# Full-precision router logits, one-pass ranks and an eight-bank first gather in a two-layer trunk

## The chip, the cores and the metric

One core of a Trainium2 chip. Five engines work side by side: TensorE (PE, matmul), VectorE (DVE), ScalarE (ACT), GpSimd (POOL) and SyncE (SP, which issues the weight DMAs). The metric is the device time of one execution in microseconds.

## What is computed

Two pre-norm residual layers over 256 tokens of width 1024. Each has a mixer of four branches and then a channel mixer: dense in layer 0, in layer 1 a top-2-of-8 mixture of experts. The change lies between the mixer of layer 1 and its first expert:

```python
def moe_swiglu(h, w_router, b_router, w_gate, w_up, w_down):
    xt = h.reshape(T, D)                      # h = RMSNorm(x), T = 256, D = 1024
    logits = (xt @ w_router).astype(jnp.float32) + b_router.astype(jnp.float32)
    top_logit, top_e = lax.top_k(logits, TOP_K)          # 2 of 8
    top_w = jax.nn.softmax(top_logit, axis=-1)
    ...
    # tokens sorted by expert; for expert e: (silu(xb @ w_gate[e]) * (xb @ w_up[e])) @ w_down[e]
    out = jnp.zeros((T, D), h.dtype).at[row_tok].add(ys * row_w[:, None].astype(ys.dtype))
```

## The kernel before

Tokens lie in two tiles of 128 (m). Nearly every product runs as three float32r products of a high and a low part (`mm3`, L390 to L392): weights land in a ring of SBUF slots by SP's DMAs (L416), ScalarE rounds each half of a piece to `whi` (`split_hi`, L371), VectorE subtracts for `wlo` (`split_lo`, L378), and six buffers of each are in turn. One half is six instructions of 512 columns on TensorE. Activations are treated alike: PSUM to `hTh` on ScalarE, the difference `hTl` on VectorE. Each engine runs its own list in program order, and semaphores join the lists.

Between the mixer and the experts of layer 1 the lists are these.

- `token_norm(3, ...)` on VectorE (L1511, L1513) adds the mixer's result to x and multiplies by the gain, in four quarters (m, g); TensorE turns each quarter (`transposed_h`, L588); ScalarE makes `hTh` (L1162) and the sums of squares (L1157), VectorE `hTl` (L1488). Then ScalarE takes the root (L1181), which loads an activation table first.
- `router()` on TensorE multiplies a 16-column matrix (router weights, high and low) with hTh and hTl (L954, L956, L959), ScalarE copies the result `lgT` out (L1451), a product with `fold` turns and adds the two halves (L965). VectorE adds the bias (L1884), finds the two largest of eight (L1888, L1895), compares indices (`hot`, L1900), and adds them to `member` columns in `tab` (L1902). Five float32 products with triangular and full ones give each token its rank within its expert and the counts (L972 to L976). VectorE copies them (L1906, L1907) and makes `pick`, 1 where a token's rank equals the column, one instruction per token tile and expert (`pick_tokens`, L2059).
- `first_gather()` multiplies the tokens (`htokh` from ScalarE, L1454, and `htokl` from VectorE, `token_lower`, L1911) with `pick`: 32 instructions of 256 columns (128 slots of each of two experts) into four banks (L982). Each bank, with two of the eight k, is copied by ScalarE (`gathered_upper`, L1425) and VectorE (`gathered_lower`, L2073).
- `expert_pass(0, 0, 0)` then runs: gate, up and down pieces in the order g0 g0 u0 u0 g1 g1 ..., with `act` (L2006) turned on TensorE (`turn`, L1086) after the second gate step has begun.

`idle_products` (L581) are products whose result nobody reads; they stand where TensorE would be empty. `link` in a list makes the engine wait for its own last instruction.

## Time and profile before

| | |
|---|---|
| time, median of 3 executions | 1021.17 us (1021.12 to 1021.25) |
| profiled execution, first to last instruction | 1019.3 us |
| TensorE busy | 1006.4 us, 99% |
| VectorE busy | 810.6 us, 80% |
| granted TensorE clock, mean | 1.000 |
| DMA | 257.13 MB, 252 GB/s |

The profile is one further execution with the hardware profiler; its own time is known as the span, and the runs without it are 1.9 us longer than that, which is what lies around the first and last instruction. A busy time is the union of an engine's instructions, and matmul ends are modelled and overlap the next start, so steps on TensorE are read from start to start. In a timeline row the first number is the start, the second the time until the end of the last of the merged instructions; in brackets stands how long the engine was idle before, and who ended that.

### The profile page before, as it was taken

How to read it: one execution, taken by the hardware profiler on the slowest of the kernel's cores; microseconds unless marked ns; L12 is line 12 of the kernel's file. 1: busy time of each engine (PE TensorE's matmuls, PEld its weight loads, DVE VectorE, ACT ScalarE, POOL GpSimd, SP SyncE). 2: the span in 40 equal slices, each digit the busy share in tenths (PEclk: the TensorE clock that was granted, in tenths of full speed). 3: DMA queues.
4: the chain of work that ended last, by engine and by line, in shares of the span. 5: the costliest groups of instructions: out<-in, count | busy, mean ns of one | idle time of the engine just before them, and what ended most of it. 6: DMA issues, size and time to landing. Idle time of an engine off the chain costs nothing.

```text
span 1019.3 us, 14045 instructions
## 1 busy us (share of the span) xinstructions
PE 1006.4 (99%) x4954; PEld 850.9 (83%) x4954; DVE 810.6 (80%) x1108; ACT 649.8 (64%) x890; POOL 38.3 (4%) x87
## 2 busy tenths in 40 slices
PE   7999999999999999999999999999999999999998
PEld 6888888888888888888888888888888988898887
DVE  5799888665645455699888858999889988989898
ACT  6657655555534343756674548787877787868775
POOL 6000000040000000100000000000000000000020
PEclk9999999999999999999999999999999999999999
DMA  9834555687455654843555556999999999999995
GB/s 273 247 113 165 162 182 169 210 242 244 168 185 191 203 170 136 284 148 121 192 160 192 186 171 217 337 373 382 364 340 395 380 364 352 391 371 356 361 394 200
DMA packets 117700, 257.13 MB, mean 252 GB/s; under 512 B 5216, under 2 KB 29858, under 8 KB 117648
## 3 DMA queue, kind: packets, MB, share of 16 engines
q1 hardware_dynamic: 113344, 243.55, 68.4%
q0 software_dynamic: 3296, 9.22, 3.1%
q10 hardware_dynamic: 1008, 3.67, 0.9%
q8 instruction: 32, 0.52, 0.2%
q14 instruction: 20, 0.16, 0.0%
HBM read 249.08 MB, written 7.34 MB: 252 GB/s over the span
## 4 chain that ended last, share of the span: by engine, by line
PE 88%; DVE 6%; ACT 3%; DMA 2%; issue 1%; SPq 0%; DVEq 0%; ACTq 0%
PE bank L390 27%; PE bank L392 26%; PE bank L391 26%; DVE wlo L378 2%; DMA ring<-in_w_in 2%; ACT whi L371 1%; DVE dacc L1723 1%; PE bank L1086 1%; PE bank L1009 1%; PE bank L1008 1%; PE bank L674 1%; DMA ring<-in_moe_w_gate 1%; PE bank L664 1%; PE bank L912 0%; PE bank L689 0%
## 5 line engine op out<-in xcount | busy, mean ns | idle before, releaser
L378 DVE TENSOR_TENSOR wlo<-ring,whi 128x1024 fp32r<-128x1024 f32 (+2 forms) x506 | 541.5, 1122 | 104.4 <-ACT whi L371 102.1
L371 ACT CAST whi<-ring 128x1024 fp32r<-128x1024 f32 (+2 forms) x506 | 463.3, 971 | 96.0 <-PE bank L392 79.0
L390 PE MATMUL bank<-whi,hTh 128*128 128x512 f32 (+3 forms) x992 | 375.4, 378 | 1.7 <-DVE wlo L378 0.9
L392 PE MATMUL bank<-whi,hTl 128*128 128x512 f32 (+3 forms) x992 | 370.4, 373 | 0.0
L391 PE MATMUL bank<-wlo,hTh 128*128 128x512 f32 (+3 forms) x992 | 370.1, 373 | 0.0
L390 PEld LDWEIGHTS bank<-whi,hTh 128*128 128x128 f32 x992 | 186.4, 188 | 32.0 <-issue 2.3
L392 PEld LDWEIGHTS bank<-whi,hTl 128*128 128x128 f32 x992 | 186.4, 188 | 29.1
L391 PEld LDWEIGHTS bank<-wlo,hTh 128*128 128x128 f32 x992 | 186.5, 188 | 28.3 <-issue 0.5
L390 PE MATMUL bank<-whi,oTh 128*128 128x512 f32 x392 | 155.4, 396 | 0.1
L392 PE MATMUL bank<-whi,oTl 128*128 128x512 f32 x392 | 153.1, 391 | 0.0
L391 PE MATMUL bank<-wlo,oTh 128*128 128x512 f32 x392 | 152.9, 390 | 0.0
L390 PEld LDWEIGHTS bank<-whi,oTh 128*128 128x128 f32 x392 | 73.7, 188 | 15.7 <-DVE wlo L378 0.7
L392 PEld LDWEIGHTS bank<-whi,oTl 128*128 128x128 f32 x392 | 73.6, 188 | 15.7
L391 PEld LDWEIGHTS bank<-wlo,oTh 128*128 128x128 f32 x392 | 73.7, 188 | 14.4
L1723 DVE SCALAR_TENSOR_TENSOR dacc<-zpad,cw,dacc 128x256 f32<-128x256 f32 x120 | 49.0, 480 | 0.0
L1250 ACT ACTIVATE gsig<-bank,rstd 128x512 f32<-128x512 f32 x32 | 20.3, 685 | 35.6 <-PE bank L392 35.4
L1383 ACT CAST oTh<-bank 128x512 fp32r<-128x512 f32 (+1 forms) x24 | 13.2, 551 | 39.2 <-PE bank L1086 39.1
L1361 ACT CAST oTh<-bank 128x512 fp32r<-128x512 f32 x11 | 6.0, 590 | 29.0 <-PE bank L912 29.0
L572 POOL DMA_INDIRECT htokh<-yrows,trowi x2 | 2.2, 1107 | 568.5 <-DVE trowi L1982 568.2
L1849 DVE SCALAR_TENSOR_TENSOR act<-bank,rstd,sig 128x512 f32<-128x512 f32 (+1 forms) x12 | 7.9, 702 | 17.6 <-PE bank L392 17.6
L1858 DVE TENSOR_TENSOR oTl<-bank,oTh 128x512 fp32r<-128x512 f32 x11 | 7.1, 687 | 18.5 <-ACT oTh L1361 18.5
L1999 DVE TENSOR_TENSOR oTl<-bank,oTh 128x512 fp32r<-128x512 f32 (+1 forms) x24 | 15.4, 643 | 7.1 <-ACT oTh L1383 6.9
(333 smaller groups left out, 678.9 us busy)
## 6 DMA issues: line engine op xcount, KB each, us to landing
ring<-in_w_in SPq DMA_DIRECT2D x40, 1024.0 KB, 5.2
ring<-in_moe_w_down SPq DMA_DIRECT2D x40, 1024.0 KB, 7.0
ring<-in_moe_w_gate SPq DMA_DIRECT2D x32, 1024.0 KB, 6.9
ring<-in_moe_w_up SPq DMA_DIRECT2D x32, 1024.0 KB, 7.8
ring<-in_moe_w_gate SPq DMA_DIRECT2D x16, 768.0 KB
ring<-in_moe_w_up SPq DMA_DIRECT2D x16, 768.0 KB, 7.2
ring<-in_ffn_w_gate SPq DMA_DIRECT2D x11, 1024.0 KB, 5.1
ring<-in_ffn_w_up SPq DMA_DIRECT2D x11, 1024.0 KB, 5.1
```

What stands on the lines that cost most here:

```text
L371: nc.scalar.copy(whi[pc.part(hf)][:, 0:n], pc.raw[:, hf * n:(hf + 1) * n]).then_inc(hi_done, 1)
L378: nc.vector.tensor_tensor(wlo[q][:, 0:n], pc.raw[:, hf * n:(hf + 1) * n], whi[q][:, 0:n].bitcast(F32), ALU.subtract).then_inc(lo_done, 1)
L390: nc.tensor.matmul(o, sh, wh, start=start, stop=False)
L391: nc.tensor.matmul(o, sh, wl, start=False, stop=False)
L392: return nc.tensor.matmul(o, sl, wh, start=False, stop=stop)
L664: nc.tensor.matmul(bank[4 + hd][:, P:384], q[:, P:T], k[:, 0:T], start=True, stop=True).then_inc(sc_mm, 1)
L674: last = nc.tensor.transpose(bank[4 + hd][:, P * j:P * (j + 1)], probs[:, hd, P * j:P * (j + 1)], ident[:, :])
L1008: nc.tensor.matmul(o, htokh[:, m, c], pick[:, m, :, :], start=(m == 0), stop=False)
L1250: nc.scalar.activation(gsig[:, j % 2, m, :], bank[2 + m][:, :], ACT.Sigmoid, scale=rstd[:, 1, m:m + 1]).then_inc(gate_sig, 1)
L1383: nc.scalar.copy(eaTh[st % 2][:, 0:n], bank[4][:, 0:n]).then_inc(e_aT_hi, 1)
L1723: ins = V.scalar_tensor_tensor(out=dacc[:, c, :], in0=z, scalar=cw[:, c, j:j + 1], in1=dacc[:, c, :], op0=ALU.mult, op1=ALU.add)
L1999: V.tensor_tensor(eaTl[st % 2][:, 0:n], bank[4][:, 0:n], eaTh[st % 2][:, 0:n].bitcast(F32), ALU.subtract).then_inc(e_aT_lo, 1)
```

## The change

The router's logits are computed by plain float32 products from unsplit turned tokens (`hTf`), with tokens as output rows, so that neither the copy nor the fold is needed. `last_norm` takes the place of `token_norm(3, ...)` on ScalarE: the square root's table is loaded first, token tile 1's squares are summed in halves, and the PSUM copies are shared between ScalarE (three) and VectorE (two). Ranks use float32r matrices, and a token that is not a member gets its rank moved by -1024, so that no member factor is needed and the first pick is one comparison with the ranks in PSUM. The first gather writes each k to a bank of its own and is drained in eight steps. `tab` shrinks from six rows to four.

```diff
+FIRST_BANK = [2, 3, 5, 0, 1, 4, 7, 6]
+RANK0 = -1024.0
...
             def router():
-                idle_products(3)
-                pe.wait_ge(wr_lo, 1)
...
-                pe.wait_ge(lgT_ev, 1)
-                pe.wait_ge(iota_ready, 1)
-                for m in range(MT):
-                    last = nc.tensor.matmul(bank[6][:, 32 + 8 * m:40 + 8 * m], lgT[0:2 * NE, P * m:P * (m + 1)],
-                                            fold[0:2 * NE, :], start=True, stop=True)
-                last.then_inc(lgT_mm, 1)
-
-                idle_products(10)
+                def logits(m, g):
+                    pe.wait_ge(hTf_ready[m][g], 2 if m and g else 1)
+                    for k in range(4 * g, 4 * g + 4):
+                        last = nc.tensor.matmul(bank[2 + m][:, 0:NE], hTf[:, k, P * m:P * (m + 1)], wr[:, k, :],
+                                                start=(k == 0), stop=(k == KD - 1))
+                    if g:
+                        last.then_inc(lg_mm, 1)
+
+                transposed_h(3, [(0, 0), (0, 1), (1, 0)])
+                pe.wait_ge(router_in, 32)
+                logits(0, 0)
+                pe.wait_ge(h_ready, h_count(3, 1, 1))
+                for k in range(4, KD):
+                    last = nc.tensor.transpose(bank[1 if k < 6 else 7][:, P * (k % 2):P * (k % 2 + 1)],
+                                               hm[:, 1, P * k:P * (k + 1)], ident[:, :])
+                    if k % 2:
+                        last.then_inc(hT_mm, 1)
+                logits(0, 1)
+                logits(1, 0)
+                idle_products(2, 0)
+                logits(1, 1)
+                idle_products(8, 0)
+                pe.wait_ge(ranker_ready, 1)
                 pe.wait_ge(member_ready, 1)
-                mem = [tab[:, 2 + m, 0:NE] for m in range(MT)]
-                nc.tensor.matmul(bank[6][:, 0:8], upstrict[:, :], mem[0], start=True, stop=True)
-                nc.tensor.matmul(bank[6][:, 8:16], upstrict[:, :], mem[1], start=True, stop=False)
+                mem = [member[:, m, :] for m in range(MT)]
+                nc.tensor.matmul(bank[6][:, 0:8], ranker[:, :], mem[0], start=True, stop=True)
+                nc.tensor.matmul(bank[6][:, 8:16], ranker[:, :], mem[1], start=True, stop=False)
                 nc.tensor.matmul(bank[6][:, 8:16], ones[:, :], mem[0], start=False, stop=True)
                 nc.tensor.matmul(bank[6][:, 16:24], ones[:, :], mem[0], start=True, stop=False)
                 nc.tensor.matmul(bank[6][:, 16:24], ones[:, :], mem[1], start=False, stop=True).then_inc(rank_mm, 1)
-                idle_products(6)
+                idle_products(6, 0)
 
             def first_gather():
                 def product(k, tokens, m, start=False, stop=False):
-                    o = bank[(5, 6, 0, 1)[k // 2]][:, T * (k % 2):T * (k % 2) + T]
-                    return nc.tensor.matmul(o, tokens[:, m, P * k:P * (k + 1)], pick[:, m, :, :], start=start, stop=stop)
-
-                def opened(k):
-                    product(k, htokh, 0, start=True)
-                    product(k, htokl, 0)
-                    product(k, htokh, 1)
+                    return nc.tensor.matmul(bank[FIRST_BANK[k]][:, 0:T], tokens[:, m, P * k:P * (k + 1)],
+                                            pick[:, m, :, :], start=start, stop=stop)
 
                 pe.wait_ge(pick_ready, 1)
                 pe.wait_ge(tok_hi, 2)
+                for k in range(KD):
+                    if FIRST_BANK[k] == 6:
+                        pe.wait_ge(rank_read, 1)
+                    product(k, htokh, 0, start=True)
+                    product(k, htokh, 1)
                 pe.wait_ge(tok_lo, 1)
-                for part in range(4):
-                    opened(2 * part)
+                for k in range(KD):
+                    product(k, htokl, 0)
                 pe.wait_ge(tok_lo, 2)
-                for part in range(4):
-                    product(2 * part, htokl, 1, stop=True)
-                    opened(2 * part + 1)
-                    product(2 * part + 1, htokl, 1, stop=True).then_inc(gat_mm, 1)
+                for k in range(KD):
+                    product(k, htokl, 1, stop=True).then_inc(one_mm, 1)
...
-                    if side == 0 and st == 0:
-                        pe.wait_ge(gat_lo, 4 * q + 2 * part + 2)
+                    if side == 0 and st == 0 and not first:
+                        pe.wait_ge(gat_lo, 4 * q + 2 * part - 2)
                     for hf in range(2):
+                        if st == 0 and first:
...
             mixer(1)
-            transposed_h(3)
             router()
             first_gather()
-            idle_products(4)
             expert_pass(0, 0, 0)
...
+            def last_norm():
+                def turned_copy(m, g, n):
+                    act_e.wait_ge(hT_mm, h_count(3, m, g))
+                    nc.scalar.copy(hTf[:, 4 * g:4 * g + n, P * m:P * (m + 1)],
+                                   bank[h_bank(3, m, g)][:, 0:P * n].rearrange("p (k t) -> p k t", t=P)
+                                   ).then_inc(hTf_ready[m][g], 1)
+
+                nc.scalar.activation(stat[:, 62:63], eps[:, :], ACT.Sqrt)
+                act_e.wait_ge(x_new, 10)
+                nc.scalar.activation(esig, x[:, 0, :], ACT.Square, accum_out=ssum[:, 0:1])
+                act_e.wait_ge(x_new, 11)
+                link(nc.scalar.activation(eact[:, 0:512], x[:, 1, 0:512], ACT.Square, accum_out=ssum_half[:, 0:1]))
+                link(nc.scalar.activation(ssum_half[:, 1:2], ssum_half[:, 0:1], ACT.Identity, bias=eps[:, 0:1],
+                                          scale=1.0 / D))
+                turned_copy(0, 0, 4)
+                act_e.wait_ge(x_new, 12)
+                link(nc.scalar.activation(eact[:, 512:D], x[:, 1, 512:D], ACT.Square, accum_out=ssum[:, 1:2]))
+                nc.scalar.activation(rstd[:, 0, 0:1], ssum[:, 0:1], ACT.Sqrt, bias=eps[:, 0:1], scale=1.0 / D)
+                nc.scalar.activation(rstd[:, 0, 1:2], ssum[:, 1:2], ACT.Sqrt, bias=ssum_half[:, 1:2],
+                                     scale=1.0 / D).then_inc(rms_root, 1)
+                turned_copy(0, 1, 4)
+                turned_copy(1, 1, 2)
...
-            token_norm(3, after_mixer(1, 1))
-            act_e.wait_ge(lg_mm, 1)
-            nc.scalar.copy(lgT[0:2 * NE, :], bank[7][0:2 * NE, 0:T]).then_inc(lgT_ev, 1)
+            last_norm()
             act_e.wait_ge(rstd_ready, 4)
             for m in range(MT):
                 nc.scalar.mul(htokh[:, m, :], hm[:, m, :], rstd[:, 1, m:m + 1]).then_inc(tok_hi, 1)
             split_hi(act_e, after_mixer(1, 1))
             act_e.wait_ge(diff_ready, 1)
             nc.scalar.activation(wtop[:, :, :], diff[:, :, :], ACT.Sigmoid).then_inc(wtop_ready, 1)
-            for part in range(4):
-                gathered_upper(0, part, (5, 6, 0, 1)[part])
+            for k in range(KD):
+                act_e.wait_ge(one_mm, k + 1)
+                nc.scalar.copy(hTh[:, k, :], bank[FIRST_BANK[k]][:, 0:T]).then_inc(one_hi, 1)
             expert_pass(0, 0, 0)
             act_e.wait_ge(rounds_ready, 1)
...
                 elif k == 3:
-                    lower_hT(k, [(0, 0), (1, 0), (0, 1), (1, 1)])
+                    for done, b, first, n in ((15, 5, 0, 4), (17, 7, 6, 2)):
+                        dve.wait_ge(hT_mm, done)
+                        V.tensor_copy(hTf[:, first:first + n, P:2 * P],
+                                      bank[b][:, 0:P * n].rearrange("p (k t) -> p k t", t=P)
+                                      ).then_inc(hTf_ready[1][first // 4], 1)
...
             def router_prep():
                 dve.wait_ge(iota_ready, 1)
-                V.tensor_copy(iotaf[:, :], iotai[:, :])
+                link(V.tensor_copy(iotaf[:, :], iotai[:, :]))
+                V.tensor_scalar(marks[:, :], iotaf[:, :], RANK0, None, ALU.add)
                 V.memset(tab[:, :, :], 0.0)
-                dve.wait_ge(wr_hi, 1)
-                V.tensor_tensor(wrl, wr[:, :, :], wrh.bitcast(F32), ALU.subtract).then_inc(wr_lo, 1)
+                V.scalar_tensor_tensor(out=ranker[:, :], in0=ident[:, :], scalar=RANK0 - 1.0, in1=upper[:, :],
+                                       op0=ALU.mult, op1=ALU.add).then_inc(ranker_ready, 1)
 
             def router():
-                dve.wait_ge(lgT_mm, 1)
                 dve.wait_ge(rstd_ready, 4)
                 for m in range(MT):
-                    last = V.scalar_tensor_tensor(out=lg[:, m, :], in0=bank[6][:, 32 + 8 * m:40 + 8 * m],
-                                                  scalar=rstd[:, 1, m:m + 1], in1=rbias[:, :], op0=ALU.mult, op1=ALU.add)
+                    dve.wait_ge(lg_mm, m + 1)
+                    link(V.scalar_tensor_tensor(out=lg[:, m, :], in0=bank[2 + m][:, 0:NE], scalar=rstd[:, 1, m:m + 1],
+                                                in1=rbias[:, :], op0=ALU.mult, op1=ALU.add))
+                    link(V.max(top8[:, m, :], lg[:, m, :]))
+                    last = V.max_index(idx8[:, m, :], top8[:, m, :], lg[:, m, :])
                 link(last)
-                for m in range(MT):
-                    last = V.max(top8[:, m, :], lg[:, m, :])
-                link(last)
+                link(V.tensor_copy(idxf[:, :, :], idx8[:, :, 0:2]))
+                chosen = idxf[:, :, :].rearrange("p m s -> p s m")
+                link(V.tensor_tensor(hot[:, :, :, :],
+                                     iotaf[:, 0:NE].unsqueeze(1).unsqueeze(1).to_broadcast([P, 2, MT, NE]),
+                                     chosen.unsqueeze(3).to_broadcast([P, 2, MT, NE]), ALU.is_equal))
+                V.tensor_tensor(member[:, :, :], hot[:, 0, :, :], hot[:, 1, :, :], ALU.add).then_inc(member_ready, 1)
                 for s in range(2):
                     last = V.tensor_tensor(diff[:, :, s:s + 1], top8[:, :, s:s + 1], top8[:, :, 1 - s:2 - s],
                                            ALU.subtract)
                 last.then_inc(diff_ready, 1)
-                for m in range(MT):
-                    last = V.max_index(idx8[:, m, :], top8[:, m, :], lg[:, m, :])
-                link(last)
-                link(V.tensor_copy(idxf[:, :, :], idx8[:, :, 0:2]))
-                for s in range(2):
-                    for m in range(MT):
-                        last = V.tensor_scalar(hot[:, s, m, :], iotaf[:, 0:NE], idxf[:, m, s:s + 1], None, ALU.is_equal)
-                link(last)
-                V.tensor_tensor(tab[:, 2:4, 0:NE], hot[:, 0, :, :], hot[:, 1, :, :], ALU.add).then_inc(member_ready, 1)
-                token_lower(0)
-                dve.wait_ge(member_ready, 1)
                 dve.wait_ge(rank_mm, 1)
+                rank = bank[6][:, 0:2 * NE].rearrange("p (m e) -> p m e", m=MT)
+                V.tensor_tensor(pick[:, :, :, :], marks[:, :].unsqueeze(1).unsqueeze(1).to_broadcast([P, MT, 2, P]),
+                                rank[:, :, 0:2].unsqueeze(3).to_broadcast([P, MT, 2, P]),
+                                ALU.is_equal).then_inc(pick_ready, 1)
                 V.tensor_copy(cnt[:, :], bank[6][:, 16:24])
-                link(V.tensor_copy(tab[:, 0:2, 0:NE], bank[6][:, 0:16].rearrange("p (m e) -> p m e", m=MT)))
+                V.tensor_copy(tab[:, 0:2, 0:NE], rank).then_inc(rank_read, 1)
...
                 link(V.tensor_reduce(tpass[:, :, :], oprod[:, :, :, :], AX_X, ALU.add))
+                link(V.tensor_scalar(trank[:, :, :], trank[:, :, :], RANK0, None, ALU.subtract))
...
-                        member = tab[:, 2 + m, bass.ds(2 * q + side, 1)]
-                        last = V.tensor_scalar(pick[:, m, side, :], iotaf[:, :], rank, member, ALU.is_equal, ALU.mult)
+                        last = V.tensor_scalar(pick[:, m, side, :], marks[:, :], rank, None, ALU.is_equal)
...
             router()
-            pick_tokens(0)
-            token_lower(1)
-            split_lo(dve, after_mixer(1, 1), halves=(0,))
-            for part in range(4):
-                gathered_lower(0, part, (5, 6, 0, 1)[part])
+            for m in range(MT):
+                token_lower(m)
+            for k in range(KD):
+                if k == 4:
+                    split_lo(dve, after_mixer(1, 1), halves=(0,))
+                dve.wait_ge(one_hi, k + 1)
+                V.tensor_tensor(hTl[:, k, :], bank[FIRST_BANK[k]][:, 0:T], hTh[:, k, :].bitcast(F32),
+                                ALU.subtract).then_inc(one_lo, 1)
             split_lo(dve, after_mixer(1, 1), halves=(1,))
             router_weights()
```

The order on TensorE from the last transposes to the first expert weights, before (waits in brackets, rows that repeat left out):

```order
L588 MATMUL bank<-ident,h 128x128 [waits h_ready]
L588 MATMUL bank<-ident,h 128x128 x3
L581 MATMUL bank<-upper,ident 128x128 x3
L956 MATMUL bank<-hTh,wrp 16x256 [waits hT_lo,wr_lo]
L965 MATMUL bank<-fold,lgT 128x8 [waits iota_ready,lgT_ev]
L965 MATMUL bank<-fold,lgT 128x8
L581 MATMUL bank<-upper,ident 128x128 x10
L972 MATMUL bank<-tab,upstrict 128x8 [waits member_ready]
L581 MATMUL bank<-upper,ident 128x128 x6
L982 MATMUL bank<-pick,htokh 128x256 [waits tok_lo,tok_hi,pick_ready]
L581 MATMUL bank<-upper,ident 128x128 x4
L390 MATMUL bank<-whi_60,hTh 128x512 [waits lo_done,gat_lo]
```

and in the change (`L583` and `L956` are the transposes, `ym` holds the turned tokens):

```order
L946 MATMUL bank<-wr,ym 128x8 [waits hTf_ready00,router_in]
L946 MATMUL bank<-wr,ym 128x8 x3
L956 MATMUL bank<-ident,h 128x128 [waits h_ready]
L946 MATMUL bank<-wr,ym 128x8 [waits hTf_ready01]
L946 MATMUL bank<-wr,ym 128x8 [waits hTf_ready10]
L576 MATMUL bank<-upper,ident 128x128 x2
L946 MATMUL bank<-wr,ym 128x8 [waits hTf_ready11]
L576 MATMUL bank<-upper,ident 128x128 x8
L968 MATMUL bank<-member,ranker 128x8 [waits member_ready,ranker_ready]
L576 MATMUL bank<-upper,ident 128x128 x6
L977 MATMUL bank<-pick,htokh 128x256 [waits tok_hi,pick_ready]
L394 MATMUL bank<-whi_60,hTh 128x512 [waits lo_done,one_lo]
```

The first logits now stand ahead of the last four transposes, and the idle products lie around the last logits.

VectorE, from the ranks to the sixth low half, before:

```order
L1906 COPY cnt<-bank 128x8 [waits rank_mm,member_ready]
L1907 COPY tab<-bank 128x2x8
L2059 TENSOR_SCALAR pick<-iotaf,tab 128x128 [waits dve_seq]
L2059 TENSOR_SCALAR pick<-iotaf,tab 128x128 x3
L1911 SCALAR_TENSOR_TENSOR htokl<-h,rstd,htokh 128x1024 [waits tok_hi]
L378 TENSOR_TENSOR wlo_68<-ring_56,whi_62 128x1024 [waits hi_done]
L2073 TENSOR_TENSOR hTl<-bank,hTh 128x512 [waits gat_hi] x4
L378 TENSOR_TENSOR wlo_69<-ring_56,whi_63 128x1024 [waits hi_done]
```

and in the change:

```order
L1920 TENSOR_TENSOR pick<-marks,bank 128x512 [waits rank_mm]
L1923 COPY cnt<-bank 128x8
L1924 COPY tab<-bank 128x2x8
L1928 SCALAR_TENSOR_TENSOR htokl<-h,rstd,htokh 128x1024 [waits tok_hi] x2
L2120 TENSOR_TENSOR hTl<-bank,hTh 128x256 [waits one_hi] x4
L382 TENSOR_TENSOR wlo_68<-ring_56,whi_62 128x1024 [waits hi_done]
L2120 TENSOR_TENSOR hTl<-bank,hTh 128x256 [waits one_hi] x4
L382 TENSOR_TENSOR wlo_69<-ring_56,whi_63 128x1024 [waits hi_done]
```

Both token halves moved behind the comparison, and the low weight half `wlo_68` from ahead of the drain into its middle.

## Rows read from the trace of the kernel before

**Rows 1.** The page: span, and TensorE's busy tenths in 40 slices.

```profile
span 1019.3 us, 14045 instructions
...
PE   7999999999999999999999999999999999999998
```

**Rows 2.** Windows: length, busy us and instructions of PE, PEld, DVE, ACT, POOL, clock, DMA.

```profile
612.40:629.40 17.00, 15.47 (x126) 13.79 (x124) 13.43 (x38) 12.97 (x20) 0.00 (x0) 1.00 0.59 221
629.40:643.10 13.70, 13.70 (x63) 11.28 (x63) 13.48 (x18) 11.50 (x12) 0.00 (x0) 1.00 0.79 284
```

**Rows 3.** The chain of waits: start us, us, what.

```profile
616.93 1.28 ACT L1181
...
619.43 2.43 PE bank L581 x20
...
623.46 1.12 DVE pick L2059 x4
...
624.62 4.10 PE bank L982 x32
```

**Rows 4.** Timeline of PE, from the fold products to the gather.

```profile
618.82 0.61 PE L965 MATMUL bank<-fold,lgT 16*128 16x8 f32 x4 [0.73 <-ACT lgT L1451]
...
621.78 0.39 PE L972 MATMUL bank<-tab,upstrict 128*128 128x8 f32 x2
622.03 0.37 PE L973 MATMUL bank<-tab,upstrict 128*128 128x8 f32 x2
...
622.92 1.58 PE L581 MATMUL bank<-upper,ident 128*128 128x128 f32 x12
```

**Rows 5.** Timeline of DVE, from the last h to the tokens' low part.

```profile
613.84 0.69 DVE L1513 TENSOR_TENSOR h<-x,gain 128x512 f32<-128x512 f32 x1
...
619.47 0.36 DVE L1884 SCALAR_TENSOR_TENSOR lg<-bank,rstd,rbias 128x8 f32<-128x8 f32 x2 [0.75 <-PE bank L965]
...
620.49 0.16 DVE L1895 FIND_INDEX8 idx<-top,lg 128x8 uint32<-128x8 f32 x1
620.68 0.17 DVE L1897 CAST idxf<-idx 128x4 f32<-128x4 uint32 x1
...
621.55 0.18 DVE L1902 TENSOR_TENSOR tab<-hot 128x16 f32<-128x16 f32 x1
...
624.49 1.28 DVE L1911 SCALAR_TENSOR_TENSOR htokl<-h,rstd,htokh 128x1024 fp32r<-128x1024 f32 x1
```

**Rows 6.** Timeline of ACT: copies, root, first copy of the gather.

```profile
613.04 1.56 ACT L1162 CAST hTh<-bank 128x512 fp32r<-128x512 f32 x3 [0.70 <-PE bank L588]
...
618.22 0.30 ACT L1181 ACTIVATE rstd<-ssum,eps 128x2 f32<-128x2 f32 x1
...
626.96 2.39 ACT L1425 CAST hTh<-bank 128x512 fp32r<-128x512 f32 x4 [2.62 <-PE bank L982]
```

**Rows 7.** Timeline of DVE, from the drain to the first activation product.

```profile
627.58 2.49 DVE L2073 TENSOR_TENSOR hTl<-bank,hTh 128x512 fp32r<-128x512 f32 x4 [0.68 <-ACT hTh L1425]
629.99 1.22 DVE L378 TENSOR_TENSOR wlo<-ring,whi 128x1024 fp32r<-128x1024 f32 x1
...
631.91 9.41 DVE L378 TENSOR_TENSOR wlo<-ring,whi 128x1024 fp32r<-128x1024 f32 x8
641.24 0.68 DVE L2006 TENSOR_TENSOR act<-sig,bank 128x512 f32<-128x512 f32 x1
```

**Rows 8.** Groups by line and form, ACT: count, busy us, mean ns, idle before.

```profile
L1402 ACT CAST pickT<-bank 128x256 fp32r<-128x256 f32 x1 | 0.4, 373 | 2.1 <-PE bank L1018 2.1
```

**Rows 9.** Timeline of PE: the first weights and the first expert transposes.

```profile
629.37 0.47 PE L390 MATMUL bank<-whi,hTh 128*128 128x512 f32 x1
...
643.09 0.60 PE L1086 MATMUL bank<-ident,act 128*128 128x128 f32 x4
```

**Rows 10.** Timeline near the end, DVE and PE's weight load.

```profile
979.22 0.17 DVE L1969 TENSOR_SCALAR tover<-trank 128x4 f32<-128x4 f32 x1
...
1002.90 0.19 PEld L390 LDWEIGHTS bank<-whi,oTh 128*128 128x128 f32 x1 [0.42 <-DVE wlo L378]
```

79 lines of the change are left out of this document (29 added, 50 removed).

## The prediction

> **What bounds the kernel now.** I read the page first: a span of 1019.3 us and a TensorE row that is full in every slice but the first and the last [rows 1]. Such a row hides short holes, so I then took the two stretches around the change by windows [rows 2]. From 612.4 to 629.4 TensorE computes no weights at all: it transposes, routes, gathers and runs idle products. This 17.0 us is the only place that the change can shorten much. From 629.4 to 643.1 TensorE is busy for all of 13.7 us, and VectorE for 13.48 of them. That second number matters more than the first: whatever is won before 629.4 must be followed by a VectorE that has 0.2 us to spare.
>
> The granted clock is 1.00 in both stretches. Ten half pieces of six weight products each fill 629.37 to 643.09 [rows 9], 1.37 us for one.
>
> **What is removed or moved.** Square-root table load: 1.28 us stood between the second square sum and the root [rows 3]. In the change it is issued before any x of this norm is ready, where ScalarE idles. The chain through 16-row logits, their copy to SBUF and the fold products is gone; so are four hTh/hTl splits that only served the router. Ten rank instructions become five. Four picks (1.12 us) and two copies ahead of them become one comparison. Four idle products before the first weights go, two are added between the logits, two fewer stand before the ranks. Against this stand 16 new logit products in float32, two instructions each if they act as the old rank products [rows 4], and a gather that is drained in eight narrow steps instead of four wide ones.
>
> **The new chain, on the old trace's clock.** Up to the last h, which ends at 614.53 [rows 5], nothing changes.
>
> - ScalarE: the first half square of token tile 1 can start at 612.51, when its x is ready; with the accumulator read it ends at 613.2. A small activation (0.2, taken like the root's 0.30 less one column and a wait) and the copy of (0,0), 0.59 as in [rows 6], end at 614.07. The second half square, its read and two roots (each starts 0.2 after the one before [rows 6]) end at 615.1, the copy of (0,1) at 615.70.
> - TensorE: logits (0,0) from 614.12. Eight instructions at 0.112: the old rank products with 8 columns start 0.25 apart once and 0.22 afterwards, for two instructions [rows 4]. They end at 615.02, so the last four transposes, which could go at 614.58 before, wait 0.44 behind them. (0,1) must wait for the copy and starts at 615.75; (1,0) follows at once; 16 instructions, to 617.54. Two idle products, 0.53. (1,1) from 618.07, the last instruction at 618.85 and its result at 619.10.
> - VectorE then does the token tile 1 alone, since tile 0 is done by 617.5: logits 0.22, maximum 0.17, match and find 0.23, cast 0.17, one comparison of 32 columns 0.19, member 0.18 [rows 5], and 0.03 to 0.04 at each of five waits. Member stands at 620.5.
> - Idle products: eight are 16 instructions. In the old chain 20 such instructions took 2.43 us, 0.121 each [rows 3], so they occupy TensorE until 620.9. They run 0.35 us longer than what they bridge.
> - Ranks: 5 x 0.112, the last result at 621.60. The comparison of 512 columns from PSUM is bounded by 0.68 (one subtraction of this size from PSUM, [rows 7]) and by 1.12 (the four old picks, [rows 3]). I take 0.69, since it is one instruction of the same shape: ready at 622.4. But six idle products take 1.42 [rows 4] and hold TensorE until 622.9. Another 0.5 us of waiting that the change makes itself.
> - Gather: 24 instructions at 0.12 (32 took 4.1 us in the chain, [rows 3]) before the first bank gets its last one: 625.86, result 626.14. The two low halves of the tokens, 1.28 each [rows 5], now both stand behind the comparison and end at 624.9, in time.
> - First copy out of PSUM: at 626.18, where the old one started at 626.96 [rows 6]. **Here the gain is 0.8 us**, although the route to it looks much shorter.
>
> **The drain and what it does to VectorE.** A copy of 256 columns is 0.37 on ScalarE [rows 8]; the first low part starts at 626.57. On VectorE the start-to-start time is 0.60 for 512 columns and 1.14 for 1024 [rows 7]; that is 0.067 per instruction and 1.04 ns per column, so 0.333 for 256. TensorE needs two of the eight: it starts weights at 627.37 against 629.37 [rows 9], **2.0 us earlier**. VectorE however must do all eight and one weight half between them, 8 x 0.333 + 1.14 = 3.8 us, and so reaches the next half at 630.37. It was 629.99 before: 0.4 us *later*. Its small weight columns (1.92 from that start to the next half) are the same in both, so the eight halves that began at 631.91 begin at 632.29. There was one wait of 0.14 among them, on a ScalarE that is now ahead; without it the activation product, 641.24 before, starts at 641.47 and ends at 642.15. The first expert transposes need it. They ran at 643.09 [rows 9]; now they can run at 642.20.
>
> So TensorE, 2.0 us ahead at first, loses 0.2 at the fourth half, 0.5 at the fifth (634.9 before, which is 629.37 and four halves; it could start at 632.9 and its low half ends at 633.5), and 0.4 at the transposes. **What is left is 0.9 us.** Behind them every half has over 2 us in hand in the old trace, so this shift lasts: TensorE has no idle time to give or lose until the end.
>
> At the end the change adds one small VectorE operation with a wait, 0.19 us, ahead of 979.22 [rows 10]. VectorE is nearly full from there to 1002.90, where TensorE waits for a low half. I book 0.1 us (0 to 0.19; a wait of 0.14 in front of that half may take it up). The extra constants of the first layer and the removed pool work lie where TensorE does not wait for them; nothing. Dropping the member factor changes no duration: both forms read at least one scalar column.
>
> Sum: 0.9 - 0.1 = 0.8 us off the profiled execution, span 1018.5 for 1019.3. The runs show 1021.17, that is 1.9 more than the span, in a spread of 0.13; with the same offset 1020.4. About 0.2% (2.0 us) is what a measurement of this kernel can tell from no change.
>
> The Trainium skill has a rule against the eight narrow steps. "VectorE: DVE Perf Modes", section on the TRN2 errata, charges every operation a fixed latency (120 cycles from PSUM) and advises tiles of 512 or more. By its table eight steps of 256 columns cost 0.5 us more than four of 512, and the sum would fall to an estimated 0.6 us. Above, rows of this case give 0.27 for the same difference, and the sum goes by them.
>
> **Rivals.**
>
> - *VectorE does not hold TensorE, and the idle products do not overhang.* Speaks for it: 2.0 us at the first weights is a plain result, and both overhangs (0.35 + 0.5) are estimates from 0.121 per instruction. Against: VectorE was busy 13.48 of 13.70 us [rows 2]. If the full head start survives, 2.0 + 0.85 - 0.1 = 2.75: 1018.4. With only the overhangs gone and VectorE still in the way, 1.65: 1019.5, inside my range. 0.11.
> - *TensorE's clock falls (slower).* Between 615.7 and 622.4 the change leaves TensorE 24 instructions with 8 columns each, 5 rank ones and idle products; before, most of this time held products with 256 columns. For it: the columns per us are the lowest of this whole stretch. Against: the old trace has a hole of 0.73 us and then 8-column instructions here [rows 4], at a granted clock of 1.00 [rows 2]. If the clock drops to 1.2 GHz at logits (1,1) and is back for the gather, 8 + 16 + 5 + 12 instructions cost twice: +0.9 +1.9 +0.6 +1.4 = 4.8 us, 1025.2. It decides the sign from about 8 such instructions on, and is measurable from 25. 0.08.
>   The Trainium skill, "TensorE: Matmul & The Clock Gate", in its part on PE-mode transpose, says that a transpose does not count as busy for the clock gate in the way a product does; by that rule the fall would be likelier and its price the same. No row decides it: the old trace has 16 transposes in this stretch at a clock of 1.00.
> - *The change does not do what it says.* The comparison with two broadcast operands, one in PSUM, or the accumulator reads with their waits cost more than their nearest rows, by 0.5 us or more together. Then VectorE starts the eight halves a whole microsecond late and nothing is left: 1021.0 to 1021.5. 0.08.
>
> **How the numbers follow.** Forecast 0.73: 0.3 (0.121 for all small instructions, tail 0.19) to 1.7 us off. The range 1019.2 to 1021.3 holds this and most of the last rival, and leaves out the first two, 0.19. Faster by over 0.2% is the first rival, 0.11; slower is the clock, 0.08; all else is within 0.2%, 0.81.
>
> **What would show it.** In the new profile: no table load before the root; first weights near 627.4 but the first expert transposes only near 642.2; before them TensorE waits for VectorE at the low halves and at the activation product; idle products directly followed by ranks and by the gather, without a wait on member or pick. I am wrong if TensorE does not wait between 627 and 643, or if the granted clock of 612 to 629 is under 1.

## Result and profile after

The change is slower by 0.23%: 1022.99 us against 1020.83 (medians of 12 each), a ratio of 1.0023 with an interval of 1.0016 to 1.0030. The forecast was 1020.4 in 1019.2 to 1021.3, "within 0.2%". The 12 times lie between 1020.86 and 1025.94, those of before between 1020.08 and 1021.25. That spread is the first hint: with each time comes a mean granted clock of TensorE, and it goes from 0.998 (1020.9 to 1022.0 us) down to 0.993 (1025.5 and 1025.9 us); with the kernel before it is 1.000.

The page of the profiled execution (1023.08 us) has it in one digit of the clock's row, in the slice of the change:

```profile
span 1021.3 us, 14020 instructions
...
PE   7999999999999999999999999999999999999998
...
PEclk9999999999999999999999998999999999999999
```

The same two windows as [rows 2]; the last three columns are the granted clock, DMA share and GB/s:

```profile
612.40:629.40 17.00, 16.59 (x116) 16.11 (x115) 8.28 (x24) 9.35 (x18) 0.00 (x0) 0.80 0.58 219
629.40:643.10 13.70, 12.96 (x57) 10.04 (x57) 13.57 (x21) 13.24 (x20) 0.00 (x0) 1.00 0.54 189
```

The clock of the first is 0.80 instead of 1.00, although TensorE is busy for 16.59 us of it and was busy for 15.47 before. TensorE's timeline tells where:

```profile
615.73 1.95 PE L946 MATMUL bank<-wr,ym 128*128 128x8 f32 x16
617.54 0.69 PE L576 MATMUL bank<-upper,ident 128*128 128x128 f32 x4
618.07 0.96 PE L946 MATMUL bank<-wr,ym 128*128 128x8 f32 x8
618.88 3.10 PE L576 MATMUL bank<-upper,ident 128*128 128x128 f32 x16
621.64 0.35 PE L968 MATMUL bank<-member,ranker 128*128 128x8 f32 x1
621.85 0.35 PE L969 MATMUL bank<-member,ranker 128*128 128x8 f32 x1
...
622.70 2.91 PE L576 MATMUL bank<-upper,ident 128*128 128x128 f32 x12
625.26 2.68 PE L977 MATMUL bank<-pick,htokh 128*128 128x256 f32 x16
...
630.27 0.50 PE L394 MATMUL bank<-whi,hTh 128*128 128x512 f32 x1 [0.42 <-DVE hTl L2120]
...
636.55 0.47 PE L394 MATMUL bank<-whi,hTh 128*128 128x512 f32 x1 [0.32 <-DVE wlo L382]
...
645.01 0.66 PE L1082 MATMUL bank<-ident,act 128*128 128x128 f32 x4
```

Read the starts. Eight logit instructions take 0.81 us (618.07 to 618.88), 0.10 to 0.11 each. Of the sixteen idle ones behind them the first start 0.11 apart (0.19 once); from 619.64 on two starts lie 0.213 apart. The rank products are 0.21 apart, the twelve idle instructions take 2.56 us (622.70 to 625.26). Only from 626.5, in the gather, is the old pitch back. That is 1.2 GHz for 6.8 us, and it covers the idle products that hide the router's VectorE work, so that TensorE comes to the ranks 1.2 us after `member` is ready and to the gather 1.7 us after the pick:

```profile
620.23 0.18 DVE L1913 TENSOR_TENSOR member<-hot 128x16 fp32r<-128x16 f32 x1
...
622.88 0.69 DVE L1920 TENSOR_TENSOR pick<-marks,bank 128x512 fp32r<-128x512 f32 x1 [2.33 <-PE bank L972]
...
629.46 1.42 DVE L2120 TENSOR_TENSOR hTl<-bank,hTh 128x256 fp32r<-128x256 f32 x4 [3.35 <-ACT hTh L1473]
...
635.18 9.17 DVE L382 TENSOR_TENSOR wlo<-ring,whi 128x1024 fp32r<-128x1024 f32 x8
644.27 0.68 DVE L2024 TENSOR_TENSOR act<-sig,bank 128x512 f32<-128x512 f32 x1
```

Up to there all went by the forecast: `member` at 620.41 (620.5 forecast), and one comparison of 0.69. First weights came at 630.27 against 629.37 before, first expert transposes at 645.01 against 643.09 [rows 9]: 1.9 us later, and the span is 2.0 longer.

Executions start up differently (the last h ends anywhere between 612.9 and 614.5), so from here on milestones are counted from the end of the last h. Counted like this they repeat closely: a second trace of before (run `before_again`) has the transposes at 28.55, the first has them at 28.56. The table gives us after the last h:

| | before | change | wide_packed | wide_relief | combined | packed |
|---|---|---|---|---|---|---|
| member ready | 7.20 | 5.98 | 6.08 | 6.08 | 5.63 | 5.63 |
| first gather product | 10.10 | 10.84 | 8.15 | 8.14 | 7.25 | 7.25 |
| first ACT copy out of PSUM | 12.44 | 14.63 | 11.41 | 11.42 | 10.55 | 10.55 |
| first expert weights | 14.85 | 15.85 | 12.63 | 12.63 | 11.76 | 11.76 |
| first expert transposes | 28.56 | 30.58 | 27.36 | 26.37 | 25.50 | 25.50 |
| end of the last VectorE addition to x | 402.21 | 404.35 | 401.08 | 400.56 | 399.41 | 399.01 |

### The profile page after: what moved, and what is told of

It reads as the page before. It is cut to its first block, busy times and chain, and to the rows that moved or that the text cites. A ratio compares the mean times of both kernels' runs of the same rounds, so it can differ in the third digit from the quotient of the medians.

```text
span 1021.3 us, 14020 instructions
## 1 busy us (share of the span) xinstructions
PE 1009.6 (99%) x4947; PEld 853.7 (84%) x4947; DVE 807.8 (79%) x1106; ACT 649.6 (64%) x896; POOL 37.4 (4%) x82
## 4 chain that ended last, share of the span: by engine, by line
PE 85%; DVE 8%; ACT 3%; DMA 2%; issue 1%; SPq 0%; DVEq 0%; ACTq 0%
PE bank L394 26%; PE bank L396 26%; PE bank L395 26%; DVE wlo L382 4%; DMA ring<-in_w_in 2%; ACT whi L375 1%; DVE dacc L1741 1%; PE bank L1082 1%; PE bank L576 1%; PE bank L1002 1%; PE bank L1003 1%; PE bank L669 1%; DMA ring<-in_moe_w_gate 1%; PE bank L659 1%; PE bank L907 0%
```

## Experiments

Unless it says otherwise a run has 5 to 11 timed executions beside the kernel before on the same chip (median there 1020.02 to 1020.49), and its edit is made to the changed kernel.

### What lowers the clock

`wide`: the logits' moving operand becomes 128 columns wide.

```diff
-        wr = place("wr", [P, KD, NE])
+        wrw = place("wrw", [P, KD * NE + 120])
+        wr = wrw[:, 0:KD * NE].rearrange("p (k e) -> p k e", e=NE)
...
+            nc.gpsimd.memset(wrw[:, KD * NE:KD * NE + 120], 1.0).then_inc(pool_seq, 1)
...
-                        last = nc.tensor.matmul(bank[2 + m][:, 0:NE], hTf[:, k, P * m:P * (m + 1)], wr[:, k, :],
+                        last = nc.tensor.matmul(bank[2 + m][:, 0:P], hTf[:, k, P * m:P * (m + 1)],
+                                                wrw[:, NE * k:NE * k + P],
```

> Theory C: the clock falls because the 32 logit instructions move only 8 columns each past a full weight load. Here the moving operand has 128 columns (the 8 router columns and 120 that nobody reads), so each instruction stays at 0.112 to 0.12 us. C expects a granted clock of 1.00 in 612 to 629, no pitch of 0.213 in the idle products, the first expert weights at about 627.5, the first expert transposes at about 642.3, a time of 1020.2 to 1020.6 and the narrow spread of the kernel before. Theory H: the holes and the transposes ahead of the logits let it fall, whatever the logits look like. H expects the fall as in the change, a median near 1023.0 and single times between 1020.9 and 1025.9.

Measured: 1019.67 us, ratio 0.9997 (0.9988 to 1.0006); clock 1.00 in the profile and 0.999 or 1.000 in all 11 executions, times from 1019.28 to 1020.29. The start-to-start time is still 0.112 with 128 columns. `member` comes 0.10 later (6.08 against 5.98), and the idle products hide that. Theory C holds; H, as a cause whatever the logits look like, is out: the same transposes and holes, no fall.

`wide_no_table` takes the early square root away from it, so that the table loads in the path again.

```diff
-                nc.scalar.activation(stat[:, 62:63], eps[:, :], ACT.Sqrt)
```

> The wide logits, without the early square root, so that the table loads ahead of the first root again, 1.28 us in the trace of before. It stands ahead of copy (0,1), so logits (0,1), (1,0), (1,1), member, ranks, gather and first weights come 1.2 to 1.3 us later (member 7.3 us after the last h against 6.08) and the time rises by 1.2 to 1.3: about 1020.9. The hole of 1.4 us before logits (0,1) may lower the clock as well; then the mean clock is under 0.999 and the time over 1022. Rival: the table is loaded elsewhere anyway, or the root is off the path, and nothing changes.

Measured: 1021.16, ratio 1.0009 (1.0000 to 1.0018), clock 1.00 in 10 of 11 and 0.999 in one. `member` at 7.38 (6.08), transposes at 28.67 (27.36): 1.3 us, the table's price. TensorE's timeline shows that a hole, even ahead of all this, did not lower the clock:

```profile
616.76 2.05 PE L948 MATMUL bank<-wrw,ym 128*128 128x128 f32 x16 [1.23 <-ACT ym L1183]
```

`more_idle2`: narrow logits, more idle products among them.

```diff
+                idle_products(2, 6)
                 logits(0, 1)
+                idle_products(2, 6)
                 logits(1, 0)
-                idle_products(2, 0)
+                idle_products(4, 6)
```

> The change as it is, with six more idle products among the narrow logits: two ahead of (0,1), two ahead of (1,0), four instead of two ahead of (1,1). Theory C (sparse and narrow work lowers the clock, dense work among it holds it): the granted clock stays at 1.00 or falls later and for less than the 6.8 us of the change; cost of the fillers 1.1 to 1.3 us on the way to logits (1,1), given back only in part by the slack of VectorE, so 1020.8 to 1021.5 in all runs. Theory W (only the 128-column operand inside the logits can hold it): the fall comes as in the change and the time is about 1024.

Measured: 1020.44, ratio 1.0010 (0.9997 to 1.0023). Ten of 11 executions at a clock of 0.999 or 1.000, one at 0.993, which took 1027.51. Dense work among the narrow products helps too, but less surely, and costs 1.08 us on the way (transposes 28.45 against 27.36 in `wide`). The same edit with the six products written to bank 0 (`more_idle`) has no time.

`combined_narrow` is `combined` (below) with 8 columns again:

> The combined version (low half ahead of the drain, 7 and 4 idle products, none ahead of logits (1,1)) with the logits 8 columns wide again: the only difference to it is the width of the moving operand. Theory C: the clock falls to 0.5 before member is known, in most runs, for 4 to 14 us; ranks, idle products and gather run at 0.21 each; mean clock 0.993 to 0.998 and a median of 1020 to 1022 against 1017.95. Rival: the fall in the change came from its two idle products standing between the logits or from where the drain stood, and the clock stays at 1.00, with a time of 1017.7 to 1018.2.

Measured: 1020.06, ratio 0.9997 (0.9988 to 1.0006), 1018.35 to 1022.05, and a mean clock of 0.995 to 0.998 in every one of 11 executions. The windows and then three rows of TensorE:

```profile
612.40:619.00 6.60, 6.19 (x46) 5.71 (x45) 3.43 (x11) 6.15 (x14) 0.00 (x0) 0.87 1.04 393
619.00:626.00 7.00, 7.00 (x34) 7.00 (x34) 4.27 (x14) 2.42 (x3) 0.00 (x0) 0.50 0.37 135
626.00:629.40 3.40, 3.40 (x25) 3.40 (x24) 1.28 (x2) 0.33 (x2) 0.00 (x0) 0.78 0.00 0
```

```profile
615.77 3.06 PE L946 MATMUL bank<-wr,ym 128*128 128x8 f32 x20
618.68 3.33 PE L576 MATMUL bank<-upper,ident 128*128 128x128 f32 x14
...
624.44 3.51 PE L976 MATMUL bank<-pick,htokh 128*128 128x256 f32 x16
```

So the width of one operand is worth 2.1 us between the medians of these two kernels, or 0.0018 of the ratio to the kernel before (1.8 us). What comes along with the width in `combined` is the extra 120 columns: they are set once at the start, and they move the tiles behind them. That is not what holds the clock: `wide_packed` (below) takes 120 columns that are there anyway, leaves the tiles behind them where they were, and has a clock of 1.00 too.

`before_thin`: the kernel before without `idle_products(3)` and `idle_products(10)` in its router.

> The kernel before without the three idle products ahead of the router and the ten behind the fold products; its logits are 24 instructions of 256 columns. TensorE then stands empty for about 0.75, 0.7 and 2.4 us between 615 and 621.7. If gaps alone lower the clock, it falls to 0.5 for the ranks, the idle six and the gather: 1023 to 1026. If it needs narrow instructions rather than gaps, the clock stays at 1.00 and the time at 1020.8.

Measured: 1022.7, ratio 1.0024 (1.0014 to 1.0035), clock 0.996 to 0.998 in all 8.

```profile
617.76 0.61 PE L964 MATMUL bank<-fold,lgT 16*128 16x8 f32 x4 [0.74 <-ACT lgT L1449]
620.72 0.60 PE L970 MATMUL bank<-tab,upstrict 128*128 128x8 f32 x2 [2.36 <-DVE tab L1900]
621.17 0.57 PE L971 MATMUL bank<-tab,upstrict 128*128 128x8 f32 x2
```

Two rank instructions take 0.43 to 0.45, against 0.22 to 0.25 in [rows 4]. So gaps lower the clock as well: it fell at 619.4, 1.0 us into the wait of 2.36 us, and was back at 626.2. The idle products of the kernel before did more than pass the time. My prediction read its clock of 1.00 as a sign of robustness; without 13 of its idle products this kernel does not keep it.

`after_again`: the change unaltered, one execution.

> The change once more. Its 12 times lie between 1020.9 and 1025.9 at mean clocks of 0.998 to 0.993. Theory C: the fall begins at the same place (behind logits (1,1), some 5 us after the last h) but lasts differently, 4 to 14 us, and the delay at the first expert transposes against the wide logits (27.36) is near half of its length.

Measured: 1022.62. The place is not fixed:

```profile
615.16 2.42 PE L946 MATMUL bank<-wr,ym 128*128 128x8 f32 x16
617.44 1.20 PE L576 MATMUL bank<-upper,ident 128*128 128x128 f32 x4
618.43 1.71 PE L946 MATMUL bank<-wr,ym 128*128 128x8 f32 x8
620.00 3.59 PE L576 MATMUL bank<-upper,ident 128*128 128x128 f32 x16
```

Here the logits (1,1) already take 1.57 for 8; the fall came at 616.5, during (1,0), and the full clock was back at 623.3, just before the ranks. With that `member` is at 7.68, but the delay at the transposes is the same (30.62 against 30.58). The fall covered 6.8 us in both traces and 10.2 in `combined_narrow`; "same place, varying length" was wrong on the place.

### Whether VectorE holds TensorE behind the first weights

`wide_relief`: the wide logits, and the low half of the first expert weights ahead of the drain instead of in its middle.

```diff
+            split_lo(dve, after_mixer(1, 1), halves=(0,))
             for k in range(KD):
-                if k == 4:
-                    split_lo(dve, after_mixer(1, 1), halves=(0,))
```

> As the wide logits, and the low half of the first expert weights (1.14 us on VectorE) stands ahead of the eight drain steps instead of in their middle. Theory V, the prediction's: VectorE, with 0.2 us to spare, hands its lateness on to TensorE (0.2 + 0.5 + 0.4). VectorE idles between the low token half (624.9) and the first low part (626.5), so the half costs nothing there, and V expects no stalls at the low halves and the transposes: 1.0 to 1.1 us less than with the wide logits alone, 1019.2 to 1019.5. Rival: TensorE waits for something else there (ScalarE's high halves or the ring), and the two kernels are within 0.2.

Measured: 1018.79, ratio 0.9987 (0.9978 to 0.9996). First weights at the same 12.63, transposes 26.37 against 27.36: 0.99 less, as theory V says. In the window TensorE's missing time is back, first `wide` and then here (the last h of this trace ends 1.3 us earlier, so the windows do not hold quite the same work; from the first weights to the transposes it is 13.74 us, ten halves of 1.37):

```profile
629.40:643.10 13.70, 13.35 (x59) 10.24 (x58) 13.63 (x18) 10.89 (x13) 0.00 (x0) 1.00 0.80 289
```

```profile
629.40:643.10 13.70, 13.70 (x64) 11.37 (x63) 13.70 (x14) 11.48 (x14) 0.00 (x0) 1.00 0.99 344
```

`relief_trim`: that, with fewer idle products.

```diff
-                idle_products(8, 0)
+                idle_products(7, 0)
...
-                idle_products(6, 0)
+                idle_products(4, 0)
```

> Wide logits, low weight half ahead of the drain, and one idle product fewer ahead of the ranks (7), two fewer ahead of the gather (4). The profile with 8 and 6 shows ranks 0.16 us after member and the gather 0.47 after the pick is ready. Theory O (idle products overhang what they bridge): 0.5 to 0.6 us less than with 8 and 6, first weights 12.1 us after the last h (12.63 there). Rival G: three idle products fewer are enough to lower the clock; then the gather and the ranks run at 0.21 each and the time is 2 to 4 us above that.

Measured: 1018.37, ratio 0.9984 (0.9975 to 0.9993), clock 1.00; first weights 12.21, transposes 25.93, so 0.44. Nearly all is the gather's overhang; the one product ahead of the ranks gave 0.02.

`wide4`: as `wide_relief`, but four banks with two k each, drained in four steps of 512.

```diff
-FIRST_BANK = [2, 3, 5, 0, 1, 4, 7, 6]
+FIRST_BANK = [2, 3, 5, 0]
...
-                    return nc.tensor.matmul(bank[FIRST_BANK[k]][:, 0:T], tokens[:, m, P * k:P * (k + 1)],
+                    return nc.tensor.matmul(bank[FIRST_BANK[k // 2]][:, T * (k % 2):T * (k % 2) + T],
+                                            tokens[:, m, P * k:P * (k + 1)],
```

> Wide logits and low half ahead of the drain, but the first gather goes back to four banks with two k each, drained in four steps of 512 columns. If the eight banks carry part of the gain, first weights or transposes come later than with eight (12.63 and 26.37 us after the last h). My sums from 0.60 for a step of 512 on VectorE: low half at 11.35, drain 11.7 to 14.1 against 14.5 with eight, first weights at 12.7 to 12.8 since the gather ends with all four products of a k. So transposes 26.4 to 26.6 and the time within 0.2 us of that with eight banks: the drain in eight steps is worth nothing either way. Rival: one finished bank at a time holds ScalarE's high halves up, +0.5 or more.

Measured: 1018.82, ratio 0.9987 (0.9978 to 0.9996); first weights 12.77, transposes 26.37, to 0.01 the same as with eight banks. The eight banks win nothing as soon as VectorE is not in the way.

`wide_old_pick`: the wide logits, with two copies and four picks in place of the comparison.

```diff
-                V.tensor_tensor(pick[:, :, :, :], marks[:, :].unsqueeze(1).unsqueeze(1).to_broadcast([P, MT, 2, P]),
-                                rank[:, :, 0:2].unsqueeze(3).to_broadcast([P, MT, 2, P]),
-                                ALU.is_equal).then_inc(pick_ready, 1)
                 V.tensor_copy(cnt[:, :], bank[6][:, 16:24])
-                V.tensor_copy(tab[:, 0:2, 0:NE], rank).then_inc(rank_read, 1)
+                link(V.tensor_copy(tab[:, 0:2, 0:NE], rank))
+                V.engine_nop().then_inc(rank_read, 1)
+                pick_tokens(0)
```

> The wide logits with two copies and four picks in place of the one comparison in PSUM. Durations of before (picks start 0.65 after the last rank product starts, 1.12 for four) put the pick 0.78 us later, 8.44 after the last h. But six idle products hold TensorE until 8.14 now, so the gather starts at 8.5 against 8.14: only 0.3 to 0.4 us on first weights and transposes. Rival: all 0.78 is seen, because the low token halves behind the pick (2.56 us) end later than the gather needs them: 24 products take 2.9 from its start, the halves would end 11.0 after the last h against 11.4 needed, so I give this little.

Measured: 1019.72, ratio 0.9993 (0.9984 to 1.0002). The pick is ready 0.48 later, the gather starts 0.07 later (8.20 against 8.14), transposes 0.07 later. The idle products hide nearly all of it. Smaller than I expected, because the four picks now take 0.87 instead of the 1.12 of [rows 3]:

```profile
621.66 0.87 DVE L2077 TENSOR_SCALAR pick<-marks,tab 128x128 fp32r<-128x128 f32 x4
```

### Where the lead goes behind the transposes

`before_again` and `wide_again`, one execution each on one chip:

> The kernel before once more, for a second trace on the same chip as the next two. The first trace has 402.2 us from the last h to the end and 373.65 of them behind the first expert transposes; versions with wide logits have 373.9 to 374.5 there. If the tail takes part of the gain, this trace repeats 373.65 within 0.1; if such sums scatter by 0.4 from execution to execution, it does not.

> The wide logits once more: first weights 12.6 and transposes 27.4 after the last h as in its first trace, clock 1.00; the part behind the transposes tells with the kernel before of this chip how much of the 1.2 us is lost behind them.

Measured, from the first expert transposes to the end of the last VectorE addition: before 373.65 and 373.69, wide 374.04 and 374.48. The 1.20 us at the transposes repeat (27.36 both times); 0.8 and 0.4 of them arrive. One part is a wait of TensorE for a low half near 1002, which changes from execution to execution; in `wide_again` it is:

```profile
1002.49 0.50 PE L395 MATMUL bank<-whi,oTh 128*128 128x512 f32 x1 [0.49 <-DVE wlo L383]
```

The other part, 0.3, grows evenly over the expert passes: the transposes of the last one stand 350.79 and 350.85 behind the first in the two traces of before, 351.16 and 351.21 with the wide operand, and 350.8 with narrow logits (`more_idle2`). The extra 120 columns had moved every tile behind them by 480 bytes. Over all traces: 351.04 to 351.24 in the nine with that shift, 350.72 to 350.88 in the nine without it, the two of the change and the two packed ones among them.

`wide_packed`: the router's 64 columns directly ahead of the constant `upper`.

```diff
-        upper = place("upper", [P, P])
+        wrw = place("wrw", [P, KD * NE + P])
+        wr = wrw[:, 0:KD * NE].rearrange("p (k e) -> p k e", e=NE)
+        upper = wrw[:, KD * NE:KD * NE + P]
```

> The wide logits with the same sums, but the 8 router columns stand directly ahead of the constant upper in one tile, so the 120 unread columns are upper's and no tile of the rest of the program moves; with the first form everything behind wr lies 480 bytes further. In six traces of wide forms the expert passes behind the first transposes (to the turned activations of the last pass) take 350.9 to 351.2 on the way to the last ones against 350.8 before and 350.8 with narrow logits. Theory A (placement in SBUF costs 0.3): 350.75 to 350.8 here, first weights and transposes as in the wide form (12.6 and 27.36), time 0.3 lower, near 1019.6. Rival S (another cause that goes with the wide products): 351.1 again.

Measured: 1019.55, ratio 0.9990 (0.9981 to 0.9999); 350.78. Theory A holds. This is the change with its clock held and next to nothing else touched: `upper` and the four small tiles behind it lie 256 bytes further than in the change, all others where they were. Its windows and the waits of TensorE in them:

```profile
619.00:626.00 7.00, 7.00 (x63) 7.00 (x63) 4.47 (x15) 3.09 (x6) 0.00 (x0) 1.00 0.40 146
...
629.40:643.10 13.70, 13.35 (x59) 10.26 (x58) 13.63 (x18) 10.92 (x13) 0.00 (x0) 1.00 0.78 282
```

```profile
626.79 0.50 PE L395 MATMUL bank<-whi,hTh 128*128 128x512 f32 x1 [0.42 <-DVE hTl L2121]
...
633.08 0.47 PE L395 MATMUL bank<-whi,hTh 128*128 128x512 f32 x1 [0.30 <-DVE wlo L383]
```

### A version that beats both

`combined`: `relief_trim`, and no idle products between the logits:

```diff
-                idle_products(2, 0)
                 logits(1, 1)
                 idle_products(7, 0)
```

> Wide logits, low half ahead of the drain, 7 and 4 idle products, and none of the two ahead of logits (1,1), whose copies stood 1.3 us before TensorE came to them (616.20 against 617.54 in the change). Expected: a further 0.45 us before member, so 1.0 us below the version with 8, 6 and 2: a ratio to the kernel before of about 0.9975 to 0.9980. Rival G: with dense work gone from between the logits the clock falls, and the time is at or above the kernel before. Rival V2: VectorE or the ring's DMAs become the bound behind the first weights and the last 0.5 us is not seen.

Measured: 1017.95, ratio 0.9979 (0.9969 to 0.9988), clock 1.00; `member` 0.45 earlier, transposes 25.50.

`combined_tail`: without the operation that takes `RANK0` back.

```diff
-                link(V.tensor_scalar(trank[:, :, :], trank[:, :, :], RANK0, None, ALU.subtract))
-                V.tensor_scalar(tover[:, :, :], trank[:, :, :], float(SLOTS) - 0.5, None, ALU.is_gt)
+                V.tensor_scalar(tover[:, :, :], trank[:, :, :], float(SLOTS) - 0.5 + RANK0, None, ALU.is_gt)
```

> The combined version without the small VectorE operation that takes RANK0 back from the ranks near 978: the constant is put into the comparison's threshold and into the product behind it. The prediction booked 0.1 us (0 to 0.19) for it. Theory T: VectorE bounds the chain into the low half near 1000, where TensorE waits 0.31, and 0.1 to 0.19 us come back: that wait shrinks to 0.15 to 0.25. Rival: the wait hangs on the drain of x and on a DMA, and neither it nor the time changes (1017.95 plus or minus 0.3 either way, so the trace decides).

Measured: 1017.51, ratio 0.9975 (0.9966 to 0.9985), but the last addition ends at 399.45 against 399.41, and the late wait is 0.03 shorter, where theory T expected 0.06 to 0.16. No gain is shown for the operation; the difference of the ratios is within their intervals.

`packed`: both, with the operand of `wide_packed`.

> Everything together: packed wide logits, low half ahead of the drain, 7 and 4 idle products, none ahead of logits (1,1), no extra operation in the tail. Transposes 25.5 us after the last h as in the combined version; with theory A another 0.3 behind them: a ratio of 0.997 to the kernel before (0.9975 without), 1017.2 to 1017.5.

Measured: 1016.78 (1016.68 to 1017.43, 5 executions), ratio 0.9964 (0.9951 to 0.9978), the last addition ends at 399.01. It is 3.7 us under the kernel before (1020.49 there), and 0.4 to 0.7 lower than expected.

## Why the prediction was wrong

- **The clock: the step that failed.** "Eight instructions at 0.112", "0.121 each" and all the rest of the new chain took a full clock for granted; the fall was the second rival, at 0.08, "against: the old trace has a hole of 0.73 us and then 8-column instructions here, at a granted clock of 1.00". That row could not carry this weight. Before it stood 16 products with 256 columns and behind it 20 idle instructions, and with the idle ones taken out this same kernel falls. The change put 32 instructions of 8 columns in their place. The rival named the right mechanism, and the place to within 2 us (logits (1,1), 3.5 us after the last h; the falls began 5.2 and 2.6 after it). The second sign that I gave for being wrong, a clock under 1 between 612 and 629, is what came: 0.80. Its price of 4.8 us was too high: measured, the change against `wide_packed`, 3.2 at the first weights and 3.2 at the transposes. In the first trace the logits (1,1) and six of the sixteen idle instructions were over when the clock fell; 10 idle ones, 5 for the ranks, 12 idle ones and the first 5 of the gather took 0.1 each more, which gives 3.2. The miss is of the same size: 2.2 us slower instead of 0.8 faster.
- **The Trainium skill's rule on transposes.** I had weighed the Trainium skill's "TensorE: Matmul & The Clock Gate", part on PE-mode transpose. The runs don't show it as the cause: `wide` has the same 16 transposes and keeps 1.00. No run takes the transposes away, so whether they add to the fall is open. The same page of the Trainium skill, section "Why this matters for your kernels", advises for throughput to keep TensorE busy; by the windows' busy column the change was busier than the kernel before (16.59 of 17.00 us against 15.47), and its clock fell.
- **Chain to the first copy: right, a little too slow.** Forecast 0.78 earlier, 1.03 in `wide_packed`. The idle instructions start 0.112 apart when the clock is full and not 0.121 (the 2.43 us that I divided by 20 ran to the end of the last one), so the overhang ahead of the ranks is 0.16 and not 0.35. That ahead of the gather is 0.47 (0.5).
- **First weights 2.0 us earlier: right** (2.22). Eight narrow drain steps start 0.332 apart on VectorE, as taken (0.333), against 0.60 for four wide ones in `wide4`: 0.26 us for the difference, where the sum had 0.27.
- **VectorE holds TensorE: right.** Forecast 0.2 at the fourth half, 0.5 at the fifth and 0.4 at the transposes; measured 0.13, 0.48 to 0.50 and 0.17 to 0.20, and behind the first two of these waits another 0.08 each, since the instruction that waited starts its successor 0.31 later and not 0.23. What is left at the transposes is 1.20, forecast 0.9. `wide_relief` takes the cause away and gets 0.99 back.
- **"Dropping the member factor changes no duration": wrong.** Four picks with one scalar column take 0.87, with two 1.12.
- **Tail 0.1: about right.** 373.72 in `wide_packed` against 373.65 and 373.69. That the operation charged for it is the cause is not shown: `combined_tail` leaves it out and its end does not come earlier.
- **Sum.** With the clock held, `wide_packed` is 0.1% below before (0.9 us, interval 0.1 to 1.9). The forecast was 0.8. In the trace the last addition ends 1.13 earlier (402.21 against 401.08), 0.3 more than forecast, and most of that is the 0.25 at the first copy. It was the right sum for another kernel. It also started from 1021.17, the median of 3 executions; that of 12 is 1020.83.

## What to carry to other kernels

A granted clock of 1.00 in the old trace belongs to the instructions that stand there. A change that replaces wide products on TensorE by narrow ones, or removes idle work, has to be priced at both clock levels, and a wide spread of times with a mean clock under 1 is the sign to look for. Where instructions start no further apart with more columns (0.112 with 8 and with 128 here), unread columns beside the few that count cost next to nothing (0.10 us once, hidden here) and kept the clock; put them where no other tile moves. And when work is brought forward on one engine, ask which engine has 0.2 us to spare behind it: nearly half of the first weights' lead (1.0 of 2.2 us) was lost there, and moving one VectorE instruction into an idle stretch gave 1.0 us.

## What the runs showed of the hardware

- Float32 instructions with 128x128 weights start 0.112 us apart at the full clock, with 128 columns (`wide`) as with 8 (the change). At half clock both idle and rank instructions are 0.213 apart.
- 32 instructions with 8 columns, with TensorE idle for only 0.4 to 0.5 us of the 17.0 around them, were followed or interrupted by 1.2 GHz in both traces of the change and in that of `combined_narrow`, and by a mean clock under 0.999 in all timed executions of both kernels; with 128 columns a hole of 1.23 us did not do it. Without narrow logits gaps did it, the last 2.36 us (`before_thin`, all 8 executions). The falls lasted 6.8 us (three traces, `before_thin` among them) and 10.2.
- A tile layout shifted by 480 bytes went with 0.3 to 0.4 us more over 351 us of expert passes. `wide` also sets its extra columns once at the start, which `wide_packed` does not; which of the moved tiles minds, and why, was not tried.
